# Retention's turned output blocks in two halves, a split third tile, another order in the LRU's last turn, and SiLU as one operation

## The chip, the cores and the metric

The kernel runs on one core of a Trainium2 chip (trn2). The metric is the device time of one execution in microseconds (us). The text speaks of the tensor engine (PE), the vector engine (DVE), the scalar engine (ACT), GpSimd (POOL) and the engine that issues the weight transfers (SP). Each engine takes its instructions in order and waits for the others through semaphores.

## What is computed

Two decoder layers over 1024 tokens of width 1024, all in float32. Layer 0 mixes tokens by retention (4 heads, keys of 256, values of 512), layer 1 by a gated linear recurrence, the LRU (width 1536, 8 gate blocks of 192). Each mixer is followed by a SwiGLU feed-forward part (FFN) of hidden width 2816. Cut to what matters here:

```python
# retention, per head
o = inner + cross                                  # (1024, 512)
o = o * rsqrt(mean(o * o) + eps)
y = (o.reshape(B, S, H * dv) * silu(g)) @ w_out

# recurrence, per channel
gate, u = split(h @ w_in)
u = conv4(u) + conv_b
r = sigmoid(blocks(u) @ w_r + b_r);  i = sigmoid(blocks(u) @ w_i + b_i)
a = exp(-8 * softplus(-lam) * r)
hs = scan(a, sqrt(1 - a * a) * (i * u))            # along the tokens
y = (hs * gelu(gate)) @ w_out

# FFN
y = (silu(h @ w_gate) * (h @ w_up)) @ w_down
```

## The kernel before

**How a product is done.** Float32 accuracy is made of three fast matmuls. Each operand is split into an upper part (`_hi`, a rounded copy) and a lower part (`_lo`, the rest), and `three` (L720 to L728) multiplies hi by hi (L724), lo by hi (L727) and hi by lo (L728) into one PSUM bank. So every operand passes two engines first: for activations ACT copies the upper part and DVE subtracts it from the source, for weights POOL (L531, L533) or ACT and POOL (L1422 or L1433, then L564) do. In the FFN both operands are also combined by sums and differences, so that seven products stand for eight (`H_Q11` to `H_Q21`, `PRODUCTS = 7`).

**Order.** Nothing is scheduled by a planner: the order on each engine is the order in which the code issues the instructions there. Two counting semaphores tie PE to the readers of its eight PSUM banks: `psum_full` counts results that PE has finished, `psum_free` counts results that have been read, and a job numbered e waits until job e - 8 is free (`free`). The reader's count goes up in the order in which DVE works, so PE's numbers must follow DVE's order.

**Retention, per head** (`head`, L886 on PE, L1345 on ACT, L1869 on DVE). PE makes q and k, the gate, the scores, the values, and then eight output blocks o(0) to o(7) of 128 tokens (18 matmuls for the last one). Each block goes to ACT for its sum of squares (L1383) and to DVE for the gate's product (L1943). After four blocks the root is taken (L1391, L1953) and `norm_o` scales the four (L1955). Then PE turns the eight blocks (L964, four 128x128 transposes a block), ACT copies the upper halves (L1395), DVE makes the lower ones (L1969), and the out projection (8 weight units, each 8 blocks of three matmuls) multiplies them. DVE adds its results to the residual (L1867). The last head's out projection is done by halves of the tokens (`out_by_halves`, L762), so that the norm and the transposes of the FFN (L1014, `early_transposes`) can start inside it.

**The recurrence** takes 384 channels a turn, four turns (`GROUPS`). In a turn PE multiplies into u (three tiles of 128 channels by 1024 tokens), into the gate, then the group before's out projection (`lru_outof`), then the gates r and i (`lru_gates`, 84 matmuls). DVE makes the convolution, then the lower half of u (`u_split`, L2272), ACT its upper half (L1648). The gates' results go through `gate_chain` in six items of 512 tokens: sigmoids on ACT (L1658, L1663), `gated` on DVE (L2282), which frees two banks an item, then `scans` (L2290, L2293, the scan itself L2298, the product with the gate branch L2303) in pairs of items, then the split of y (ACT L1690, DVE L2308). In the last turn the out projection of the group before is cut in two: its first column half (8 blocks, 72 matmuls) stands before the gates, its second half behind them; DVE's adds of the second half are placed between the steps of `gate_chain` through `meanwhile`:

```python
scans((2, 3))
meanwhile((0, 1))
y_split((2, 3))
meanwhile((2, 3))
scans((4, 5))
meanwhile((4,))
y_split((4, 5))
meanwhile((5, 6, 7))
```

Then the last group's own out projection follows by halves.

**FFN chunk.** Eleven chunks of 256 hidden columns, two tiles each (`first_tiles_up` for the first chunk of a layer, `tile` for the others). silu(x) is made as sigmoid(x) on ACT (L1445, L1449) and a product x * sigmoid(x) on DVE (L2101 and L2123 in the first chunk, L2165 and L2175 in the others), then a product with the up branch. In the first chunk of a layer ACT also rounds the weights of the down projection, in the same queue as the activations.

## Time and profile before

| what | value |
|---|---|
| median of 3 runs | 2731.73 us (2730.6 to 2732.26) |
| the profiled execution, its own time | 2731.25 us |
| its span in the profile | 2729.4 us |
| PE busy with matmuls | 2677.2 us, 98% of the span |
| DVE, ACT, POOL busy | 1341.4, 824.5, 1251.4 us |
| mean granted PE clock | 0.997 |

The span runs from the first to the last profiled instruction; the 1.85 us between it and the execution's own time lie outside. The profile gives for each engine the time in which it worked and, for each idle stretch, the instruction that ended it. Where PE is busy nearly all the time, the places at which PE waits are the ones to look for; the idle time of the other engines matters only there.

### The profile page before, as it was taken

What the parts mean: (1) busy time and instruction counts of PE and PEld (TensorE: products, weight loads), DVE (VectorE), ACT (ScalarE), POOL (GpSimd) and SP (SyncE); (2) the same over time, 40 slices, a digit from 0 to 9 for tenths busy, and PEclk for the clock granted to TensorE, in tenths of its full rate; (3) what the DMA queues carried; (4) which work ended last, traced back from release to release, by engine and by line L of the source; (5) the groups of instructions that cost most, each with busy time, mean ns of one, the idle gap of its engine ahead of it and who ended that gap; (6) DMA issues with size and microseconds to landing.
All of it is one profiled execution on the core that took longest, in us unless ns stands there. A gap on an engine that the chain in (4) does not pass through costs nothing.

```text
span 2729.4 us, 35372 instructions
## 1 busy us (share of the span) xinstructions
PE 2677.2 (98%) x12017; PEld 2214.7 (81%) x12017; DVE 1341.4 (49%) x1814; ACT 824.5 (30%) x1380; POOL 1251.4 (46%) x1204
## 2 busy tenths in 40 slices
PE   8999999999999999999999999999989999999998
PEld 6888888888888788888888788787877888888886
DVE  8333332323324855555454637356577544545555
ACT  3120120120124433333332524325265222222224
POOL 4323323323323456555555445253454556655554
PEclk9999999999999999999999999999999999999999
DMA  4102102101111111111211111111111111111212
GB/s 141 43 27 65 40 30 64 43 31 60 49 32 43 55 55 46 46 51 55 63 50 56 30 47 49 36 57 36 47 47 47 51 52 52 46 48 54 67 50 81
DMA packets 173624, 139.29 MB, mean 51 GB/s; under 512 B 9184, under 2 KB 143456, under 8 KB 173536
## 3 DMA queue, kind: packets, MB, share of 16 engines
q1 hardware_dynamic: 171440, 133.46, 16.1%
q10 hardware_dynamic: 2096, 4.62, 0.5%
q8 instruction: 59, 0.97, 0.1%
q14 instruction: 29, 0.24, 0.0%
HBM read 132.81 MB, written 5.24 MB: 51 GB/s over the span
## 4 chain that ended last, share of the span: by engine, by line
PE 89%; DVE 6%; ACT 3%; issue 1%; DMA 0%; POOL 0%; POOLq 0%; SPq 0%; DVEq 0%; ACTq 0%
PE ps L724 29%; PE ps L728 29%; PE ps L727 29%; DVE f_h_lo L2016 1%; DVE uc L2298 1%; DVE residual L1867 0%; DVE residual L2211 0%; DVE gate_buf L2303 0%; DVE residual L2369 0%; PE ps L803 0%; DVE h_sum_a L2005 0%; PE ps L865 0%; DVE gate_buf L2090 0%; ACT gate_buf L1237 0%; DVE uc L2293 0%
## 5 line engine op out<-in xcount | busy, mean ns | idle before, releaser
L564 POOL TENSOR_TENSOR f_w_lo<-f_raw,f_w_hi 128x512 fp32r<-128x512 f32 x270 | 354.7, 1318 | 444.5 <-ACT f_w_hi L1422 361.1
L724 PE MATMUL ps<-f_h_hi,f_w_hi 128*128 128x512 f32 x1232 | 481.6, 391 | 3.8 <-DVE f_h_lo L2016 2.1
L728 PE MATMUL ps<-f_h_hi,f_w_lo 128*128 128x512 f32 x1232 | 480.0, 390 | 0.0
L727 PE MATMUL ps<-f_h_lo,f_w_hi 128*128 128x512 f32 x1232 | 480.0, 390 | 0.0
L522 POOL TENSOR_TENSOR small<-w_raw 128x1 f32<-128x1 f32 x200 | 55.4, 277 | 822.7 <-PE ps L724 813.2
L2211 DVE TENSOR_TENSOR residual<-ps,residual 128x512 f32<-128x512 f32 x352 | 239.3, 691 | 157.2 <-PE ps L728 157.2
L724 PEld LDWEIGHTS ps<-f_h_hi,f_w_hi 128*128 128x128 f32 x1232 | 231.3, 188 | 57.8 <-issue 5.1
L724 PE MATMUL ps<-f_w_hi,f_act_hi 128*128 128x512 f32 x688 | 268.4, 390 | 3.0 <-POOL f_w_lo L564 2.8
L728 PEld LDWEIGHTS ps<-f_h_hi,f_w_lo 128*128 128x128 f32 x1232 | 231.3, 188 | 48.1
L727 PEld LDWEIGHTS ps<-f_h_lo,f_w_hi 128*128 128x128 f32 x1232 | 231.4, 188 | 47.0
L727 PE MATMUL ps<-f_w_lo,f_act_hi 128*128 128x512 f32 x688 | 268.0, 390 | 0.0
L728 PE MATMUL ps<-f_w_hi,f_act_lo 128*128 128x512 f32 x688 | 267.9, 389 | 0.0
L533 POOL TENSOR_TENSOR w_lo<-w_raw,w_hi 128x512 fp32r<-128x512 f32 x190 | 257.1, 1353 | 15.2
L1422 ACT ACTIVATE f_w_hi<-f_raw 128x512 fp32r<-128x512 f32 x246 | 154.4, 628 | 338.5 <-PE ps L728 338.4
L724 PE MATMUL ps<-h_hi,w_hi 128*128 128x512 f32 x632 | 248.3, 393 | 3.2 <-DVE uc L2282 3.2
L728 PE MATMUL ps<-h_hi,w_lo 128*128 128x512 f32 x632 | 246.4, 390 | 0.0
L727 PE MATMUL ps<-h_lo,w_hi 128*128 128x512 f32 x632 | 246.4, 390 | 0.0
L564 POOL TENSOR_TENSOR f_w_lo<-f_sum,f_w_hi 128x512 fp32r<-128x512 f32 x124 | 177.8, 1434 | 130.2 <-ACT f_w_hi L1422 122.8
L724 PE MATMUL ps<-w_hi,h_hi 128*128 128x512 f32 x528 | 206.1, 390 | 1.8 <-DVE residual L1867 1.4
L728 PE MATMUL ps<-w_hi,h_lo 128*128 128x512 f32 x528 | 205.7, 390 | 0.0
L727 PE MATMUL ps<-w_lo,h_hi 128*128 128x512 f32 x528 | 205.7, 390 | 0.0
L2163 DVE TENSOR_TENSOR gate_buf<-ps,gate_buf 128x512 f32<-128x512 f32 x120 | 82.8, 690 | 207.8 <-PE ps L728 207.1
(306 smaller groups left out, 4705.4 us busy)
## 6 DMA issues: line engine op xcount, KB each, us to landing
f_raw<-in_ffn_w_gu SPq DMA_DIRECT2D x176, 256.0 KB, 3.4
w_raw<-in_ret_w_in SPq DMA_DIRECT2D x96, 256.0 KB, 2.8
f_raw<-in_ffn_w_down SPq DMA_DIRECT2D x88, 256.0 KB, 2.8
w_raw<-in_lru_w_in SPq DMA_DIRECT2D x48, 256.0 KB, 2.9
w_raw<-in_ret_w_out SPq DMA_DIRECT2D x32, 256.0 KB, 2.6
w_raw<-in_lru_w_out SPq DMA_DIRECT2D x24, 256.0 KB, 2.6
residual<-in_x SPq DMA_DIRECT2D x8, 512.0 KB, 7.2
out_y<-residual SPq DMA_DIRECT2D x8, 512.0 KB, 2.6
```

The costliest lines, as they stand in the source:

```text
L522: nc.gpsimd.tensor_tensor(small[:, 62:63], col, col, ALU.subtract)
L533: nc.gpsimd.tensor_tensor(lo, raw[:, cut], hi.bitcast(F32), ALU.subtract).then_inc(w_ready, 1)
L564: nc.gpsimd.tensor_tensor(lo, src, hi.bitcast(F32), ALU.subtract).then_inc(f_wready, 1)
L724: m = nc.tensor.matmul(o, l_hi, r_hi, start=start, stop=False, skip_group_check=onto)
L727: nc.tensor.matmul(o, l_hi, r_lo, start=False, stop=False, skip_group_check=onto)
L728: return nc.tensor.matmul(o, l_lo, r_hi, start=False, stop=stop, skip_group_check=onto)
L1422: nc.scalar.activation(f_unit(j, last)[0], src, ACT.Copy).then_inc(f_whi, 1)
L2016: TT(H_lo[:, h_cut(form, k)], src[:, t_cut(k)], H_hi[:, h_cut(form, k)].bitcast(F32), ALU.subtract).then_inc(hn_dve, 1)
L2163: TT(t, f_bank(u, p), t, ALU.add).then_inc(f_ev, 1)
L2211: TT(X[:, c], ps[:, b * BANK:(b + 1) * BANK], X[:, c], ALU.add).then_inc(f_ev, 1)
L2298: k = nc.vector.tensor_tensor_scan(uc[:, cut(i)], r_buf[i % 4], uc[:, cut(i)], start, ALU.mult, ALU.add)
```

## The change

There are four parts.

1. **Retention.** PE turns blocks 0 to 3 before the last output block o(7) is summed, and blocks 4 to 7 after the first weight unit has been multiplied with blocks 0 to 3. ACT's and DVE's copies of the turned blocks move with them (`o_turned_upper`, `o_turned_lower`), and the turned blocks lie in `b_hi`/`b_lo` in two pieces (`OT_AT`), so that the first four can be written while scores of the late keys are still read.
2. **u's third tile** is rounded and split in two halves of 512 tokens (`U_PIECES`); the gates wait for the half that they read.
3. **The LRU.** In every turn `gated` of item 2 is issued between the two scans of the first pair. In the last turn only blocks 0 to 3 of the first column half stand before the gates, blocks 4 to 7 and the second half behind them; DVE's adds are placed in two lumps, four before the second pair of scans and eight inside the third pair. The FFN's first four transposes are placed after the third weight unit in both layers; in the LRU's layer, which has three units a half, they stood after the second.
4. **SiLU** is one ACT operation in the FFN; DVE's product with the sigmoid is gone (four instructions a chunk), and so are its semaphore counts. Retention's gate keeps its sigmoid.

```diff
+OT_AT = (0, SCORE_AT[3])
...
+U_PIECES = [(0, 0, S), (1, 0, S), (2, 0, BANK), (2, BANK, S)]
...
+def o_job(s):
+    return J_O + s + (4 if s == SB - 1 else 0)
+def t_job(s):
+    return J_O + s + (SB - 1 if s < 4 else SB)
...
                 pe.wait_ge(s_ready, h * len(SCORES) + len(SCORES))
-                for s in range(SB):
+                def values(s):
                     late = s >= CHUNK
...
-                    if s == 2:
-                        state_sum()
-                for s in range(SB):
-                    free(base + J_T + s)
-                    pe.wait_ge(o_ready, h * 8 + s + 1)
-                    for d in range(4):
-                        m = nc.tensor.transpose(bank(J_T + s, d * P, P),
-                                                R3[:, s * 512 + d * P:s * 512 + (d + 1) * P], ident[:])
-                    m.then_inc(psum_full, 1)
+                def o_turns(blocks):
+                    for s in blocks:
+                        pe.wait_ge(psum_free, base + o_job(s) + 1)
+                        pe.wait_ge(o_ready, h * 8 + s + 1)
+                        for d in range(4):
+                            m = nc.tensor.transpose(bank(J_T + s, d * P, P),
+                                                    R3[:, s * 512 + d * P:s * 512 + (d + 1) * P], ident[:])
+                        m.then_inc(psum_full, 1)
+                for s in range(3):
+                    values(s)
+                state_sum()
+                for s in range(3, SB - 1):
+                    values(s)
+                o_turns(range(4))
+                values(SB - 1)
...
+                        elif (nh, k) == (0, 0):
+                            o_turns(range(4, SB))
...
+                            if j == 0 and s == 4:
+                                o_turns(range(4, SB))
+                            if j == 0:
+                                pe.wait_ge(psum_free, base + t_job(s) + 1)
...
-            def early_transposes(layer, nh, k, nk):
-                if (nh, k) == (0, nk - 2):
+            def early_transposes(layer, nh, k):
+                if (nh, k) == (0, 2):
...
-                            if hf == 0 and m_i == 0 and tile < 2:
-                                pe.wait_ge(u_ready, 3 * g + 2 + tile)
+                            if m_i == 0 and (hf, tile) in ((0, 0), (0, 1), (1, 1)):
+                                pe.wait_ge(u_ready, len(U_PIECES) * g + 2 + tile + hf)
...
-            lru_outof(GROUPS - 2, u0 + 12, base, L_OUT, 0, a_hi, a_lo)
-            lru_gates(GROUPS - 1, base, L_RI_LAST, h_hi, h_lo)
-            lru_outof(GROUPS - 2, u0 + 12, base, L_RI_LAST + 12, 1, a_hi, a_lo)
-            def y_there(half, k):
-                pe.wait_ge(y_ready, (GROUPS - 1) * 6 + half * GT + k + 1)
-            out_by_halves(3, lo, GT, u0 + 18, h_hi, h_lo, y_there, lambda nh, k: early_transposes(1, nh, k, GT))
+            for first in (0, 4):
+                for k in range(GT):
+                    if first == 0:
+                        pe.wait_ge(y_ready, (GROUPS - 2) * 6 + k + 4)
+                        pe.wait_ge(w_ready, u0 + 12 + k + 1)
+                    w = slice(k * 512, (k + 1) * 512)
+                    for s in range(first, first + 4):
+                        e = (L_OUT if first == 0 else L_OUT_LAST - 4) + s
+                        if k == 0:
+                            free(base + e)
+                        c = k * S + s * P
+                        m = three(bank(e), a_hi[:, c:c + P], a_lo[:, c:c + P], w_hi[:, w], w_lo[:, w],
+                                  k == 0, k == GT - 1, s == (4 if k else 0))
+                        if k == GT - 1:
+                            m.then_inc(psum_full, 1)
+                if first == 0:
+                    lru_gates(GROUPS - 1, base, L_RI_LAST, h_hi, h_lo)
+            lru_outof(GROUPS - 2, u0 + 12, base, L_OUT_LAST + 4, 1, a_hi, a_lo)
...
+                    if s == 6:
+                        o_turned_upper(range(4))
...
-                nc.scalar.activation(r3(2 + u), f_bank(u, 0), ACT.Sigmoid).then_inc(f_sig, 1)
-            def sigmoid_2(n, u, first=False):
+                nc.scalar.activation(r3(2 + u), f_bank(u, 0), ACT.Silu).then_inc(f_sig, 1)
+            def silu_2(n, u, first=False):
                 act.wait_ge(f_ev, ev_at(n, u, E_C12, first))
-                nc.scalar.activation(r3(4 + u), r3(7), ACT.Sigmoid).then_inc(f_sig, 1)
+                nc.scalar.activation(r3(4 + u), r3(7), ACT.Silu).then_inc(f_sig, 1)
...
-                gate_o((5, 6, 7))
+                gate_o((5, 6))
+                o_turned_lower(range(4))
+                gate_o((7,))
...
                 def act_2(u):
                     dve.wait_ge(f_sig, 4 * n + 2 + u + 1)
-                    TT(r3(4 + u), r3(7), r3(4 + u), ALU.mult).then_inc(f_ev, 1)
-                    dve.wait_ge(f_ev, ev_at(n, u, E_G2, True))
                     TT(r3(4 + u), r3(4 + u), r3(u), ALU.mult).then_inc(f_act, 1)
...
+            def u_split(g, u_hi, u_lo, pieces=range(len(U_PIECES))):
+                for i in pieces:
+                    tile, a, b = U_PIECES[i]
+                    c = slice(tile * S + a, tile * S + b)
+                    dve.wait_ge(u_rounded, len(U_PIECES) * g + i + 1)
                     TT(u_lo[:, c], uc[:, c], u_hi[:, c].bitcast(F32), ALU.subtract).then_inc(u_ready, 1)
...
+                def scans(items, between=lambda: None, amid=lambda: None):
                     first = step.now()
...
+                    between()
...
+                        if j == 0:
+                            amid()
...
                 gated((0, 1))
-                scans((0, 1))
-                gated((2, 3))
+                scans((0, 1), amid=lambda: gated((2,)))
+                gated((3,))
                 y_split((0, 1))
                 gated((4, 5))
+                meanwhile(0, range(4, SB))
                 scans((2, 3))
-                meanwhile((0, 1))
                 y_split((2, 3))
-                meanwhile((2, 3))
-                scans((4, 5))
-                meanwhile((4,))
+                scans((4, 5), lambda: meanwhile(1, range(SB)))
...
+            def group_before_out(nh, blocks):
                 for s in blocks:
-                    add(base + L_RI_LAST + 12 + s, L_RI_LAST + 12 + s, s, 1)
-            gate_chain(GROUPS - 1, h_hi, h_lo, second_half_out)
+                    e = L_OUT_LAST - 4 + 8 * nh + s
+                    add(base + e, e, s, nh)
```

**The order on PE at the end of a head** (head 0). `b_hi,q_late_lo` is the last matmul of an output block, `ident,gate_buf` are the transposes of the normed blocks, `w_hi,b_hi` is the out projection. Before:

```order
L727 MATMUL ps<-b_lo,q_late_hi 128x512
L728 MATMUL ps<-b_hi,q_late_lo 128x512
L964 MATMUL ps<-ident,gate_buf 128x128 x32
L724 MATMUL ps<-w_hi,b_hi 128x512
L727 MATMUL ps<-w_lo,b_hi 128x512
```

and now (the 18 matmuls of o(7) stand at the first line of dots, three of the four blocks of the unit at the second):

```order
L751 MATMUL ps<-b_hi,q_late_lo 128x512
L983 MATMUL ps<-ident,gate_buf 128x128 x16
L747 MATMUL ps<-a_hi,b_hi 128x512
...
L751 MATMUL ps<-b_hi,q_late_lo 128x512
L747 MATMUL ps<-w_hi,b_hi 128x512
L750 MATMUL ps<-w_lo,b_hi 128x512
...
L983 MATMUL ps<-ident,gate_buf 128x128 x16
L747 MATMUL ps<-w_hi,b_hi 128x512
```

The first 16 transposes have moved ahead of o(7), and 12 matmuls of the first weight unit stand between o(7) and the other 16.

**The order on DVE in the last LRU turn**, from the second pair of scans on (`residual` is an add of the group before, `h_lo` a split of y). Before:

```order
L2290 SCALAR_TENSOR_TENSOR gate_buf<-mask,gate_buf 128x512
L2303 TENSOR_TENSOR gate_buf<-uc,gate_buf 128x512 x2
L1867 TENSOR_TENSOR residual<-ps,residual 128x512 x2
L2308 TENSOR_TENSOR h_lo<-gate_buf,h_hi 128x512 x2
L1867 TENSOR_TENSOR residual<-ps,residual 128x512 x2
L2290 SCALAR_TENSOR_TENSOR gate_buf<-tmp,gate_buf 128x512
...
L2303 TENSOR_TENSOR gate_buf<-uc,gate_buf 128x512 x2
L1867 TENSOR_TENSOR residual<-ps,residual 128x512
L2308 TENSOR_TENSOR h_lo<-gate_buf,h_hi 128x512 x2
L1867 TENSOR_TENSOR residual<-ps,residual 128x512 x11
```

and now:

```order
L1952 TENSOR_TENSOR residual<-ps,residual 128x512 x4
L2369 SCALAR_TENSOR_TENSOR gate_buf<-mask,gate_buf 128x512
...
L2385 TENSOR_TENSOR gate_buf<-uc,gate_buf 128x512 x2
L2390 TENSOR_TENSOR h_lo<-gate_buf,h_hi 128x512 x2
L2369 SCALAR_TENSOR_TENSOR gate_buf<-tmp,gate_buf 128x512
L2369 SCALAR_TENSOR_TENSOR tmp<-gate_buf,tmp 128x512
L1952 TENSOR_TENSOR residual<-ps,residual 128x512 x8
L2373 TENSOR_TENSOR uc<-uc,gate_buf 128x512
```

All eight adds of the second column half now stand ahead of the third pair's products and scans; before, four stood behind them.

**The order on PE inside the last group's out projection** (second half of the tokens; `w_hi` and `lru_out_hi` are weight units, the last `w_hi` row belongs to the second unit, the first `lru_out_hi` row to the third). Before:

```order
L724 MATMUL ps<-w_hi,h_hi 128x512
L727 MATMUL ps<-w_lo,h_hi 128x512
L728 MATMUL ps<-w_hi,h_lo 128x512
L1014 MATMUL ps<-ident,gate_buf 128x128 x16
L724 MATMUL ps<-lru_out_hi,h_hi 128x512
```

and now (the dots stand for the rest of the third unit):

```order
L751 MATMUL ps<-w_hi,h_lo 128x512
L747 MATMUL ps<-lru_out_hi,h_hi 128x512
L750 MATMUL ps<-lru_out_lo,h_hi 128x512
L751 MATMUL ps<-lru_out_hi,h_lo 128x512
...
L1059 MATMUL ps<-ident,gate_buf 128x128 x16
L747 MATMUL ps<-lru_out_hi,h_hi 128x512
```

The 16 transposes have moved back by one unit of 12 matmuls.

## Rows read from the trace of the kernel before

**Rows 1.** The profile's page, part 1: busy us, share of the span, instructions.

```profile
PE 2677.2 (98%) x12017; PEld 2214.7 (81%) x12017; DVE 1341.4 (49%) x1814; ACT 824.5 (30%) x1380; POOL 1251.4 (46%) x1204
```

**Rows 2.** PE's waits in the whole span: us in total, times, longest.

```profile
PE ps L724 <- DVE residual L1867: 6.0, 2, 4.6
PE ps L724 <- POOL f_w_lo L564: 4.8, 5, 1.6
PE ps L964 <- DVE gate_buf L1955: 4.3, 4, 1.1
PE ps L724 <- DVE uc L2282: 4.3, 4, 1.1
...
PE ps L724 <- DVE a_lo L2272: 2.6, 2, 1.3
```

**Rows 3.** Windows: busy us (instructions) in an undisturbed stretch; then the clock, DMA share.

```profile
1100.00:1200.00 100.00, 100.00 (x443) 82.86 (x442) 48.91 (x66) 29.67 (x47) 53.62 (x41) 1.00 0.19 58
```

**Rows 4.** Timeline of PE at head 0's end: start, us, instruction [idle before].

```profile
187.03 1.91 PE L964 MATMUL ps<-ident,gate_buf 128*128 128x128 f32 x16
190.06 1.94 PE L964 MATMUL ps<-ident,gate_buf 128*128 128x128 f32 x16 [1.12 <-DVE gate_buf L1955]
```

**Rows 5.** Timeline of PE at the last head's end.

```profile
832.72 0.47 PE L724 MATMUL ps<-w_hi,b_hi 128*128 128x512 f32 x1 [1.60 <-DVE b_lo L1969]
```

**Rows 6.** Timeline of ACT at head 0's end.

```profile
189.01 4.00 ACT L1395 ACTIVATE b_hi<-ps 128x512 fp32r<-128x512 f32 x8
```

**Rows 7.** Timeline of DVE at head 0's end.

```profile
189.42 1.68 DVE L1955 TENSOR_SCALAR gate_buf<-gate_buf,rstd 128x512 f32<-128x512 f32 x4
191.01 2.48 DVE L1969 TENSOR_TENSOR b_lo<-ps,b_hi 128x512 fp32r<-128x512 f32 x4
```

**Rows 8.** Timeline of DVE, second LRU turn, u's third tile.

```profile
1747.44 1.21 DVE L2272 TENSOR_TENSOR a_lo<-uc,a_hi 128x1024 fp32r<-128x1024 f32 x1
```

**Rows 9.** Timeline of DVE, same turn, items 0 to 2 of the gates.

```profile
1763.29 1.20 DVE L2298 TENSOR_TENSOR_SCAN uc<-gate_buf,uc 128x512 f32<-128x512 f32 x1
...
1765.59 0.69 DVE L2282 TENSOR_TENSOR uc<-uc,xn 128x512 f32<-128x512 f32 x1
```

**Rows 10.** Timeline of ACT, same turn: the second gate of item 2.

```profile
1762.06 0.68 ACT L1663 ACTIVATE xn<-ps,gc_gate 128x512 f32<-128x512 f32 x1
```

**Rows 11.** Timeline of PE in the last group's out projection.

```profile
2019.46 0.76 PE L724 MATMUL ps<-lru_out_hi,h_hi 128*128 128x512 f32 x1 [4.63 <-DVE residual L1867]
```

**Rows 12.** Windows behind that stall.

```profile
2019.40:2024.00 4.60, 4.45 (x10) 3.08 (x11) 4.60 (x8) 2.69 (x7) 4.03 (x3) 0.51 0.00 2
```

**Rows 13.** Timeline of DVE there: the add for which PE waits.

```profile
2018.63 0.68 DVE L1867 TENSOR_TENSOR residual<-ps,residual 128x512 f32<-128x512 f32 x1
```

**Rows 14.** Timeline of ACT ahead of layer 1's FFN: first copy from the fifth transposed tile.

```profile
2043.35 0.69 ACT L1466 ACTIVATE f_h_hi<-ps,cols 128x512 fp32r<-128x512 f32 x1
```

**Rows 15.** Timeline of DVE there: last split, then adds.

```profile
2048.13 0.75 DVE L2005 SCALAR_TENSOR_TENSOR f_h_lo<-ps,cols,f_h_hi 128x512 fp32r<-128x512 f32 x1 [0.41 <-ACT gate_buf L1466]
2048.80 2.47 DVE L1867 TENSOR_TENSOR residual<-ps,residual 128x512 f32<-128x512 f32 x4
```

**Rows 16.** Timeline of DVE, first FFN chunk of layer 0: product with the sigmoid.

```profile
923.51 0.69 DVE L2123 TENSOR_TENSOR gate_buf<-gate_buf 128x512 f32<-128x512 f32 x1
```

**Rows 17.** Timeline of PE there: start of the down projection.

```profile
927.17 0.50 PE L724 MATMUL ps<-f_w_hi,f_act_hi 128*128 128x512 f32 x1 [1.39 <-POOL f_w_lo L564]
```

**Rows 18.** Groups of instructions on ACT: sigmoid and GELU, busy, mean ns.

```profile
L1445 ACT ACTIVATE gate_buf<-ps 128x512 f32<-128x512 f32 x44 | 26.1, 599 | 69.0 <-PE ps L728 68.9
...
L1637 ACT ACTIVATE gate_buf<-ps 128x1024 f32<-128x1024 f32 x12 | 12.3, 1028 | 88.7 <-PE ps L728 88.7
```

**Rows 19.** Timeline of DVE, a later chunk: from the last product to its last split.

```profile
2677.75 0.69 DVE L2172 TENSOR_TENSOR gate_buf<-gate_buf,ps 128x512 f32<-128x512 f32 x1 [1.16 <-PE ps L728]
...
2679.55 1.78 DVE L2175 TENSOR_TENSOR gate_buf<-gate_buf 128x512 f32<-128x512 f32 x1
...
2683.73 1.00 DVE L2183 TENSOR_TENSOR f_act_lo<-gate_buf,f_act_hi 128x512 fp32r<-128x512 f32 x1 [0.70 <-ACT f_act_hi L1454]
```

More of the change, by code:

```diff
@@ L760, in tile_rows, with out_by_halves @@
                 rows_unit(j + 1, u + 1, 1, banks)
-            def out_by_halves(n, extra, nk, u0, l_hi, l_lo, ready, meanwhile):
+            def out_by_halves(n, extra, nk, u0, at, ready, between):
                 for half in range(2):
@@ L770, in out_by_halves @@
                                 pe.wait_ge(w_ready, u0 + j + 1)
-                            if nh == 0:
-                                ready(half, k)
                             w_h, w_l = out_unit(j, extra)
@@ L776, in out_by_halves @@
                                 b = i + (4 * nh if half == 0 else 0)
[L777 to L782 removed]
+                                if nh == 0:
+                                    ready(half, k, i)
+                                if k == 0 and (half or nh):
+                                    pe.wait_ge(psum_free, (e - 4 if half and nh else e - 8) + 1)
+                                m = three(bank(b), *at(half * 4 + i, k), w_h, w_l,
                                           k == 0, k == nk - 1, half == 0 and i == 0)
@@ L785, in out_by_halves @@
                                     m.then_inc(psum_full, 1)
-                            if half:
-                                meanwhile(nh, k)
+                            between(half, nh, k)
             def first_tiles(u0):
@@ L1108, in tile, with down @@
                         product(n, u, p)
-                def down(n, nh, k, s, w, fresh):
-                    if k == 0:
-                        pe.wait_ge(f_ev, fresh)
+                def down(n, nh, k, s, w, added=None, first=False):
+                    if k == 0 and added is not None:
+                        pe.wait_ge(f_ev, added)
+                    elif k == 0:
+                        tile_read(n, s if w is None else 2 * s + nh, first)
                     at = k * S + s * P
@@ L1137, in chunk @@
                         tile(n, 1)
-                    adds = n * F_EV + 2 * PRODUCTS
+                    adds = n * F_EV + 10
                     if last:
@@ L1161, in chunk @@
                                     acted(n, k, s)
-                                m = down(n, nh, k, s, None, adds + s + 1 if nh else tile_read(n, s, first))
+                                m = down(n, nh, k, s, None, adds + s + 1 if nh else None, first)
                                 if k or s == SB - 1:
@@ L1378, in head, with o_turned_upper @@
                 load_sqrt()
+                def o_turned_upper(blocks):
+                    for s in blocks:
+                        full(base + t_job(s))
+                        nc.scalar.activation(o_turned_all(s)[0], bank(J_T + s).rearrange("p (d n) -> p d n", d=4),
+                                             ACT.Copy).then_inc(ot_rounded, 1)
                 for s in range(SB):
-                    full(base + J_O + s)
+                    full(base + o_job(s))
                     if s >= 3:
@@ L1392, in head @@
                             .then_inc(o_root, 1)
-                for s in range(SB):
-                    full(base + J_T + s)
-                    nc.scalar.activation(b_hi[:, 0:4096].rearrange("p (d n) -> p d n", d=4)[:, :, s * P:(s + 1) * P],
-                                         bank(J_T + s).rearrange("p (d n) -> p d n", d=4), ACT.Copy)\
-                        .then_inc(ot_rounded, 1)
+                o_turned_upper(range(4, SB))
             head(0, True)
@@ L1640, in u_round @@
             def u_round(g, base, u_hi, begun=None, full_to=None):
-                for tile in range(GT):
+                for tile, a, b in U_PIECES:
                     if begun is not None and tile < 2:
@@ L1955, in norm_o, with o_turned_lower @@
                         TS(r3(s), r3(s), rstd[:, s:s + 1], None, ALU.mult).then_inc(o_ready, 1)
+                def o_turned_lower(blocks):
+                    for s in blocks:
+                        hi, lo_ = o_turned_all(s)
+                        dve.wait_ge(ot_rounded, h * 8 + s + 1)
+                        TT(lo_, bank(J_T + s).rearrange("p (d n) -> p d n", d=4), hi.bitcast(F32), ALU.subtract)\
+                            .then_inc(psum_free, 1)
                 gate_o(range(3))
```

137 lines of the change are left out of this document (72 added, 65 removed).

## The prediction

> **What bounds the kernel now.** I read the page first: PE works 98% of the span, DVE 49%, ACT 30%, POOL 46% [rows 1]. So PE is the bound, and nothing that shortens another engine's work is worth anything unless PE waits for it. In an undisturbed stretch a matmul starts every 0.227 us (443 records touch 100 us, two of them only in part) [rows 3]. The number of 512-column matmuls does not change, so the change can only win or lose PE's idle time, 52 us in all (2729.4 - 2677.2). Next I read the list of PE's waits [rows 2]: it names five that the change touches. They are 6.0 us for adds to the residual, 4.3 us for the normed output blocks, 4.3 us for `gated` (L2282), 2.6 us for the lower part of u's third tile, and part of the 4.8 us for a weight's lower part from POOL. Last came the timelines around each. An idle figure counts from the modelled end of the matmul before; seen from start to start each stop costs some 0.1 us more, because the first matmul behind it is slower (0.50 instead of 0.39 us for one, as in [rows 17]).
>
> **Retention's turns.** At the end of a head PE turns 16 tiles and can turn the next 16 only 3.03 us after the first (187.03 to 190.06) [rows 4]; 16 transposes need 1.78 us by their pitch of 0.11, so 1.25 us are lost. The chain in that time is o(7)'s square, mean, root and `norm_o` (DVE, 189.42) [rows 7], and it starts when o(7) is complete. Now 12 matmuls, 12 x 0.227 = 2.72 us, stand between o(7) and the second turn, so 3.03 - 2.72 = 0.3 us remain. Then block 4 must be copied: PE needs 0.5 us for it, ACT copies at 0.50 us a block (8 in 4.00) [rows 6], DVE splits at 0.62 (4 in 2.48) but only behind its four `norm_o` [rows 7], which end 1.04 us after the second turn begins. That gives about 2.05 us against the 1.78 of the turn: 0.3 us of a new wait, and 0.1 for the extra stop. The next blocks come at 0.62 us on DVE and are used at 0.68 (three matmuls). The first turn, ahead of o(7), needs `norm_o` of blocks 0 to 3, which ended while o(5) was summed; its copies (4 x 0.5 on ACT, 4 x 0.62 on DVE) lie beside the 18 matmuls of o(7), 4.1 us, and ahead of o(7)'s square on ACT. So three heads win 1.25 - 0.7 = 0.55 us each, 1.6 in all. In the last head PE also waits 1.60 us for the lower parts of four blocks, 1.75 by starts [rows 5]; that goes wholly, since blocks 4 to 7 are used only in the other half: 1.25 + 1.75 - 0.4 = 2.6. Together **4.2 us**; bounds are 2 (every head finds a wait of 0.6 more) and 5.5 (no new wait).
>
> **u's third tile.** In turns 2 and 3 PE waits 1.3 us for one split of 1024 columns, 1.21 us long, behind DVE's adds [rows 2, 8]. A half takes 0.62 to 0.69 [rows 7, 9], so PE goes on 0.5 us earlier: **1.0 us** in the two turns, bounds 0 and 1.2. The second half is read 42 matmuls later and costs nothing. ACT's extra instruction hides behind the adds.
>
> **`gated` inside the scans.** After the gates PE waits four times 1.1 us, once in each turn, for item 2's product [rows 2]: it ran at 1765.59, behind the second scan (1763.29) and two products [rows 9]. Its input was there at 1762.06 + 0.68 = 1762.74 [rows 10]. Now it starts when the first scan ends, at 1763.29, which is 2.3 us earlier; the wait of 1.2 us is gone in the three inner turns, 3.7 us. In the last turn the two blocks that follow take only 1.36 us, then PE needs item 3's product, which runs when it did: some 0.3 us come back, 0.9 are won. **4.6 us**, bounds 3 and 4.9. y of items 0 and 1 comes 0.6 us later and nobody waits for it.
>
> **The last turn.** PE stood 4.63 us (and 1.4 us before that, together 6.0) for adds of the second column half [rows 2, 11]: the add stood behind the third pair's scans and products and ran at 2018.63 [rows 13]. After that the granted clock was 0.51, the lower level (1.2 GHz), and 10 matmuls took 4.6 us instead of 2.3 [rows 12]. Now blocks 4 to 7 of the first half (4 blocks x 3 units x 3 = 36 matmuls, 8.2 us) have gone from ahead of the gates to behind them, and all eight adds stand ahead of the third pair's products. The results of the second half are complete 3 to 0.1 us before PE wants their banks; DVE is done with the second pair by then, and adds one in 0.62 us (4 in 2.47) [rows 15] against PE's 0.68 a block. I take all of it as won: 6.0 + 2.3 + 0.3 for two restarts = **8.6 us**; bounds 4 (half of the wait and the clock's part stay) and 9.
> What bears on the clock's 2.3 us: the Trainium skill's page "TensorE: Matmul & The Clock Gate", section "What's actually happening", says that the throttled state is the default and activity releases it, so without the stop the slow matmuls go too. By it the sum is the same only while no stop of that length remains here; if one did, its slow stretch would stay, which is what the bound of 4 says.
> Ahead of the gates the out projection now covers only 8.2 instead of 16.3 us of u's rounding and splitting. They need some 6 us (one GELU, 1.03 [rows 18], and u's first two tiles at 1.0 to 1.2 on each engine), so nothing is added.
>
> **The FFN's first transposes, layer 1.** They move back by one unit, 2.72 us, while the products behind them stay. ACT copies, squares and copies again without a gap, so its first copy of the fifth tile (2043.35) [rows 14] moves by 2.72; so does DVE's last split (2048.13) and the first add behind it (2048.80, ready at 2049.42) [rows 15]. PE wants that bank for the FFN's first product 0.5 us after that. So PE waits 2.2 us there, and since ACT's chain behind it (squares, root, scaling, first terms) sets the next turns too, the full shift comes out: **-2.7 us**. Bounds: 0 (if the chain has slack that I missed) and -3.5.
>
> **SiLU.** No such operation is in the trace. Its nearest rows are the sigmoid (599 ns for 512 columns) and GELU (1028 ns for 1024) [rows 18]; I take 0.6 us and bound it by 0.5 and 1.3. The Trainium skill's "ScalarE: Activation LUTs", section "What ACT_TABLE_LOAD costs", says one element a cycle for every function; by that it costs what the sigmoid costs, and the sum stands as it is. In the chunks of the loop PE does not wait, so 0.69 to 1.78 us less on DVE [rows 16, 19] buy nothing. In the first chunk of each layer they do: PE's 1.39 us [rows 17] were for a weight whose rounding stands on ACT behind the activation that needs the product of [rows 16]. One product less on that chain (0.7 with its wait) and another ahead of it on DVE (0.2, since then the matmul's result binds) give 0.95, and a wait of 0.2 to 0.3 behind it goes: 1.15 a layer, **2.3 us**; bounds 0.8 and 3.2. The last 20 us of the kernel are DVE's adds and the final norm, and are not touched.
>
> **Sum.** 4.2 + 1.0 + 4.6 + 8.6 - 2.7 + 2.3 = 18.0 us. The profiled execution took 2731.25, the median is 0.5 more. 2731.25 - 18.0 = 2713.25; for the median **2713.5 us**.
>
> **Rivals.**
> - *The later transposes cost nothing.* For it: DVE idles 0.41 us ahead of each split there [rows 15]. Against: it idles for ACT, which has no gap in that stretch. Then 2713.5 - 2.7 = 2710.8. Chance 0.12.
> - *The last turn keeps a stall.* DVE is the only engine for 12 adds, 3 splits and the third pair; if POOL's weight splits stretch its products (0.69 against 1.78 [rows 16, 19]), y or a bank is late again, say by 3 us, and the clock falls too (2.3): 2713.5 + 5 = 2718.5. For it: this stretch had such products before. Against: the adds, which PE needs, read PSUM and took 0.62. The Trainium skill's "SBUF — State Buffer", section "SBUF: two separate sides", calls the port of DVE and GpSimd an exclusive lock; a loser waits for a whole operation of the other. Chance 0.14.
> - *The early turns give their gain back* on the copies of blocks 4 to 7, or o(7) starts late: the first term falls from 4.2 to 1: 2716.7. Chance 0.08.
> - *Slower: SiLU is long.* In a later chunk DVE's last split ends at 2684.73, 6.98 us after the product's result [rows 19]; PE wants it 36 matmuls, 8.16 us, after the product, so about 1.0 us is free, and 1.6 to 2.7 with one product less. A SiLU beyond 2.3 to 3.4 us stops PE at the end of every chunk. To undo 18 us and 5.5 more in some 20 chunks it needs 1.2 us beyond that, 3.5 us or more: six times the sigmoid. At 4.6 us with the larger slack: 2713.5 + 20 x 1.2 = 2737.5. Chance 0.02.
> - *The change does not do what it says*: the order of the built programs shows the moved transposes, adds and `gated`, and the same number of table loads on ACT. Under 0.01.
>
> **The numbers.** The forecast has 0.64. About 0.2% (5.5 us) is what a measurement of this kernel can tell from no change. All cases but the slow SiLU lie over 10 us below 2731.73: faster 0.97, same 0.01, slower 0.02. The low end takes in the first rival and 1.5 us of the other bounds, the high end the second: 2709 to 2719.
>
> **What would show it.** PE's list of waits without `gated`, and with at most 0.4 us a head for L1955's successor; no window with a clock near 0.5 behind the last group's out projection; a new wait of about 2.2 us of the FFN's first product for an add to the residual in layer 1, and none in layer 0; 0.5 us or so left at the start of the first down projection; SiLU at 0.6 us. I am wrong if PE still waits over 3 us for one add in the last turn, if the first product of layer 1 does not wait, or if SiLU's mean is over 1.3 us.

## The result and the profile after

| | before | changed |
|---|---|---|
| median of 4 runs | 2731.84 us (2730.6 to 2732.26) | 2715.01 us (2714.54 to 2716.61) |
| profiled execution | 2731.25 us | 2714.54 us |
| its span | 2729.4 us | 2712.7 us |

The ratio is 0.994 with a 95% interval of 0.9923 to 0.9957: the change makes the kernel 16.8 us faster. The forecast was 2713.5 us with a range of 2709 to 2719. The total lies in the range, but it was not reached by the terms as they were given: one of them, the third largest, was nearly lost, and others came out larger.

The page's busy row of the changed kernel, for [rows 1]:

```profile
PE 2673.3 (99%) x12017; PEld 2212.2 (82%) x12017; DVE 1274.1 (47%) x1730; ACT 826.6 (30%) x1384; POOL 1259.5 (46%) x1204
```

PE's matmuls are the same in number and take 3.9 us less, mostly since ten of them no longer run at the slow clock [rows 12]. DVE lost 67 us of work that nobody waited for, apart from the first chunks.

PE's waits in the changed kernel, for [rows 2] (engine, what waits, line; what ended the wait; us in total, times, the longest):

```profile
PE ps L983 <- DVE gate_buf L2040: 4.5, 5, 1.0
...
PE ps L747 <- DVE a_lo L2351: 1.6, 2, 0.8
PE ps L747 <- DVE residual L1952: 1.5, 1, 1.5
...
PE ps L747 <- POOL f_w_lo L587: 0.6, 2, 0.3
PE ps L1059 <- DVE h_sum_a L2093: 0.6, 1, 0.6
...
PE ps L747 <- DVE uc L2361: 0.2, 1, 0.2
PE ps L1059 <- DVE f_h_lo L2093: 0.2, 1, 0.2
```

Of the five waits of [rows 2] four have shrunk, about as forecast: `gated` (now L2361) from 4.3 to 0.2, adds to the residual from 6.0 to a single new one of 1.5 us, u's lower part from 2.6 to 1.6, POOL's lower parts from 4.8 to 0.6 (of these, one stop of 1.80 us in the last chunk only changed its name: it is 1.89 now and put down to ACT's SiLU). The fifth has not: the wait for the normed output blocks (L2040, the successor of L1955) is 4.5 us in total, where it was 4.3.

The table splits the 16.7 us of span. A stop is counted from start to start ("by starts"): it is what two neighbouring matmuls take beyond 0.227 us, or two transposes beyond 0.13. "By the shift" means how much earlier the same instruction starts in the one trace than in the other; it also holds what lies between the stops.

| part | forecast | stops before | stops after | won |
|---|---|---|---|---|
| retention's turns | 4.2 | 1.26 + 1.17 + 1.17 + 1.26, and 1.74 in the last head | 1.15 + 1.05 + 1.06 + 1.15, three times 0.24 behind the turn, 0.92 + 0.22 in the last head | 0.3 (0.7 by the shift) |
| u's third tile | 1.0 | 2 x 1.47 | 2 x 0.94 | 1.1 |
| `gated` | 4.6 | 1.25 + 1.24 + 1.17 + 1.26 | 0.41 | 4.5 |
| the last turn | 8.6 | 1.57 + 4.79, and 2.7 by the slow clock | none | 9.1 |
| FFN's first transposes, layer 1 | -2.7 | 0.49 | 0.37 + 1.64 + 0.77 | -2.3 |
| SiLU | 2.3 | 2 x (0.34 + 1.55 + 0.24) | 2 x 0.48 | 3.3 to 3.5 |

The sum is 16.0 to 16.6. The head ends are where the forecast and the trace part. Here is the first head's end on DVE and POOL, where [rows 7] shows the end of the same chain before the change:

```profile
189.82 0.75 DVE L2028 SCALAR_TENSOR_TENSOR gate_buf<-ps,gam,gate_buf 128x512 f32<-128x512 f32 x1 [2.70 <-ACT tmp L1470]
190.49 1.00 DVE L2032 TENSOR_SCALAR ssq<-ssq 128x4 f32<-128x4 f32 x1
191.83 0.18 DVE L2038 RECIPROCAL rstd<-rstd 128x4 f32<-128x4 f32 x1 [0.34 <-ACT rstd L1480]
192.05 1.68 DVE L2040 TENSOR_SCALAR gate_buf<-gate_buf,rstd 128x512 f32<-128x512 f32 x4
```
```profile
189.48 0.61 POOL L554 CAST w_hi<-w_raw 128x512 fp32r<-128x512 f32 x1
190.18 1.29 POOL L556 TENSOR_TENSOR w_lo<-w_raw,w_hi 128x512 fp32r<-128x512 f32 x1
```

DVE's mean over four columns (L2032) took 1.00 us and ended at 191.49, just behind POOL's subtraction (190.18 + 1.29 = 191.47); it is 1.00 us in each of the four heads. Before the change it took 0.16:

```profile
188.71 0.16 DVE L1947 TENSOR_SCALAR ssq<-ssq 128x4 f32<-128x4 f32 x1
```
```profile
192.59 0.61 POOL L531 CAST w_hi<-w_raw 128x512 fp32r<-128x512 f32 x1
```

There POOL's split of that weight unit began at 192.59, behind the chain, because PE began the out projection only then; a unit's split starts when PE begins the unit two before it. The change lets PE begin the out projection right behind o(7), and with it POOL's split moved into DVE's chain. In the last head POOL goes on to further units, and `norm_o` is held up too:

```profile
831.26 3.04 DVE L2040 TENSOR_SCALAR gate_buf<-gate_buf,rstd 128x512 f32<-128x512 f32 x4
```

against 1.68 us for the same four in the first head. That gives the stop of 0.92 us between two turned blocks: the second of the four scalings alone took 1.49 us beside POOL's next subtraction, where one takes 0.48 by itself.

The last turn of the LRU is as forecast: behind the 0.41 us for `gated` there is no stop up to the FFN's transposes, and the granted clock stays at 1.00. Three windows of PE (stretch, length, busy us and instructions, granted clock, DMA share, GB/s), for [rows 12]:

```profile
2009.00:2014.00 5.00, 5.00 (x24) 1.00 0.00 0
2014.00:2019.00 5.00, 5.00 (x24) 1.00 0.00 0
2019.00:2024.00 5.00, 5.00 (x32) 1.00 0.01 3
```

### The profile page after: what moved, and what is told of

It reads as the page before. It is cut to its first block, busy times and chain, and to the rows that moved or that the text cites. A ratio compares the mean times of both kernels' runs of the same rounds, so it can differ in the third digit from the quotient of the medians.

```text
span 2712.7 us, 35233 instructions
## 1 busy us (share of the span) xinstructions
PE 2673.3 (99%) x12017; PEld 2212.2 (82%) x12017; DVE 1274.1 (47%) x1730; ACT 826.6 (30%) x1384; POOL 1259.5 (46%) x1204
## 4 chain that ended last, share of the span: by engine, by line
PE 92%; DVE 4%; ACT 2%; issue 1%; DMA 0%; POOL 0%; SPq 0%; DVEq 0%; ACTq 0%
PE ps L747 30%; PE ps L750 30%; PE ps L751 30%; DVE f_h_lo L2104 1%; PE ps L983 0%; ACT gate_buf L1318 0%; DVE residual L2289 0%; DVE residual L2451 0%; PE ps L823 0%; DVE h_sum_a L2093 0%; DVE gate_buf L2178 0%; DVE residual L1952 0%; DMA residual<-in_x 0%; ACT f_h_hi L1556 0%; DVE f_h_lo L2093 0%
```

## The experiments

Each starts from the changed kernel. Stops are by starts.

### 1. POOL held back in the heads

```diff
+                    if j == HEAD_UNITS - 6:
+                        pool.wait_ge(o_ready, h * 8 + 8)
                     split(slot, ...)
```

> The changed kernel, with one wait more: POOL starts the split of the out projection's third unit in each head only when the last of the eight normed blocks is there. In the changed kernel PE still loses 1.15, 1.05, 1.06 and 1.15 us ahead of the second turn, and the last head 0.92 and 0.22 us more inside it. Theory (the mean of the squares on DVE, 1.00 us instead of 0.16, and in the last head norm_o, 3.04 instead of 1.68, are held up by POOL's cast and subtraction that now lie beside them): the mean falls back to 0.16 us, norm_o to 1.68, PE loses 0.3 us ahead of each second turn and nothing inside the last head's; 4 x 0.85 + 1.1 = 4.5 us less, 2710.5 us. Rival (it is the later start of the chain, or PE's own restart, and POOL only happens to run there): the mean stays at 1.0 us or PE's stop stays at 1.05 to 1.15 us, time 2715 +- 1. Third way: POOL's later splits come too late for PE, new waits for w_lo behind the turn, slower than 2715.

Measured: 2710.82 us (2710.02 to 2711.83), 4.2 less than the changed kernel; ratio to before 0.9922 (0.9905 to 0.9939). The same chain in the last head, and POOL's first cast there:

```profile
828.03 0.16 DVE L2034 TENSOR_SCALAR ssq<-ssq 128x4 f32<-128x4 f32 x1
828.53 0.18 DVE L2040 RECIPROCAL rstd<-rstd 128x4 f32<-128x4 f32 x1 [0.34 <-ACT rstd L1482]
828.74 1.68 DVE L2042 TENSOR_SCALAR gate_buf<-gate_buf,rstd 128x512 f32<-128x512 f32 x4
```
```profile
830.63 0.61 POOL L554 CAST w_hi<-w_raw 128x512 fp32r<-128x512 f32 x1
```

The mean is back at 0.16 and `norm_o` at 1.68 us. PE's stops ahead of the second turn are 0.31, 0.22, 0.21 and 0.31 us, and no stop is left inside the last head's turn. The forecast's "0.3 us remain" was right for a chain without POOL. No wait for a weight appeared. By the shift the heads are 4.6 us shorter; the profiled span fell by 3.0 only, because 0.9 us were lost at the kernel's start and 0.8 from there to the LRU's entry, where the clock was low for longer (0.50 in both windows of 3 us from 1545 us on; 0.66 and 0.77 in the two from 1548 us on in the changed kernel, which gets there 3.7 us later). Nothing was edited at either place. One wait on POOL, which changes nothing else, brings back what this part lacked, so POOL's work beside DVE's chain had taken it. The Trainium skill's page "SBUF — State Buffer", section "SBUF: two separate sides", says that DVE and GpSimd share one pair of ports as an exclusive lock, taken by DVE operations in a two-port mode or with two inputs from SBUF. The traces agree for DVE's operations from SBUF to SBUF: 1.00 against 0.16 us, ending with POOL's operation; in which mode DVE ran them no run here shows. DVE's adds, which read PSUM, keep 0.69 us beside POOL (L1952, 673 to 693 ns in all its 128).

### 2. More cover in the last head instead

```diff
-                        elif (nh, k) == (0, 0):
+                        elif (nh, k) == (0, 1):
                             o_turns(range(4, SB))
```

> The changed kernel, with the last head's second turn behind two units of the out projection instead of one (12 matmuls, 2.72 us, more cover); the three first heads as they were. Theory (the second turn lacks cover for a chain that is 1.0 us longer than thought): the last head's 1.15 + 0.92 + 0.22 us go, those of the first three heads stay at 1.05 to 1.15; 2.2 us less, 2712.8 us. Rival (the copies of the blocks or the banks of the turned blocks then hold up the third unit or the fifth): part of it comes back as a wait for a bank or for b_lo, 2713.5 to 2715.

Measured: 2712.77 us (2712.29 to 2713.11), 2.2 less. All three stops of the last head are gone, while DVE is as slow as in the changed kernel:

```profile
829.86 0.99 DVE L2032 TENSOR_SCALAR ssq<-ssq 128x4 f32<-128x4 f32 x1
831.19 0.18 DVE L2038 RECIPROCAL rstd<-rstd 128x4 f32<-128x4 f32 x1 [0.34 <-ACT rstd L1480]
831.41 3.06 DVE L2040 TENSOR_SCALAR gate_buf<-gate_buf,rstd 128x512 f32<-128x512 f32 x4
```

The other heads kept 1.14, 1.06 and 1.04. So the collision can also be covered instead of removed; where the copies of the later blocks are needed late, 12 more matmuls cost nothing.

### 3. The FFN's first transposes of layer 1 back in their old place

```diff
-                if (nh, k) == (0, 2):
+                if (nh, k) == (0, 2 - layer):
```

> The changed kernel, with the FFN's first transposes of layer 1 one unit (2.72 us) earlier again, where the kernel before had them; layer 0 untouched. Theory (their later place costs what PE loses at 2026.5, 2032.7 and in part at 2045.8: 0.37 + 1.64 + 0.28 = 2.3 us): these three go and nothing takes their place, 2712.7 us. Rival (DVE's scaling of the eight half rows runs only from 2015.9 to 2021.6 us, 0.72 us each beside POOL's products, and PE would ask for the first four at 2018.0): PE waits 0.8 us or more for gate_buf at the first of these transposes, and one to two of the 2.3 us come back: 2714 to 2715.

Measured: 2714.54 us (2714.29 to 2716.54), no difference; the span is the same to the last digit, 2712.7. PE's waits show the exchange:

```profile
PE ps L1059 <- DVE gate_buf L2080: 2.0, 1, 2.0
...
PE ps L1059 <- DVE h_sum_a L2093: 0.3, 1, 0.3
```

The 1.5 us for the add are gone, and 2.0 us (2.21 by starts) stand ahead of the first transpose, for the rows that DVE scales. The rival holds: the late place alone does not explain the loss of 2.3 us.

### 4. SiLU undone

```diff
-                nc.scalar.activation(r3(2 + u), f_bank(u, 0), ACT.Silu)
+                nc.scalar.activation(r3(2 + u), f_bank(u, 0), ACT.Sigmoid)
...
+                TT(r3(2 + u), f_bank(u, 0), r3(2 + u), ALU.mult)
```

> The changed kernel, with SiLU undone (sigmoid on ACT, product on DVE, as before); the rest as changed. Theory (SiLU is worth only what PE loses in the first chunk of each layer): PE's stops of 0.34, 1.55 and 0.24 us come back there in place of one of 0.48, in both layers, 1.65 a layer, 3.3 us in all, 2718.3 us; the chunks of the loop show no new wait. Rival as predicted before the result: 1.15 a layer, 2717.3 us. Second rival (the loop's chunks had hidden waits that the product of 0.69 to 1.78 us made longer): more than 5 us, 2720 or above.

Measured: 2719.92 us (2718.57 to 2720.22), 4.9 more, where 3.3 were expected. The stops came back as 0.36, 1.58 and 0.25 us in place of 0.48 and 0.47, in both layers: 3.4 us, or 3.8 by the shift of the instructions behind them. In the profiled execution, 5.7 us longer in span, another 1.4 lie where SiLU has no part, behind the last head's turn, because the clock fell there (PE windows):

```profile
832.00:834.00 2.00, 0.90 (x6) 0.95 0.36 131
834.00:836.00 2.00, 2.00 (x11) 0.50 0.52 131
836.00:838.00 2.00, 2.00 (x9) 0.70 0.37 116
```

In the changed kernel the same windows have 1.00 throughout. The remaining 0.5 us lie at the kernel's start. Whether the clock fell in the three other executions too is not on record, so the median's 4.9 us cannot be split as surely. By the profiled pair SiLU is worth 3.3 to 3.8 us, all of it in the first chunks; the loop's chunks show no new stop, so the second rival falls although the median comes near its 5 us. How long the operation is could be read in the changed kernel's groups (busy us, mean ns), for [rows 18]:

```profile
L1534 ACT ACTIVATE gate_buf<-gate_buf 128x512 f32<-128x512 f32 x44 | 27.5, 625 | 8.4 <-DVE gate_buf L2252 5.5 <-DVE gate_buf L2202 2.9
L1530 ACT ACTIVATE gate_buf<-ps 128x512 f32<-128x512 f32 x44 | 26.1, 598 | 69.0 <-PE ps L751 68.9
```

598 ns from PSUM, where the sigmoid had 599 [rows 18]: the slow rival is out. The Trainium skill's "ScalarE: Activation LUTs", section "What ACT_TABLE_LOAD costs", says that every function takes one element a cycle; the two equal times agree with it.

### 5. The last turn's order undone

```diff
-            for first in (0, 4):
...
+            lru_outof(GROUPS - 2, u0 + 12, base, L_OUT, 0, a_hi, a_lo)
+            lru_gates(GROUPS - 1, base, L_RI_LAST, h_hi, h_lo)
...
-                meanwhile(0, range(4, SB))
                 scans((2, 3))
+                meanwhile((0, 1))
                 y_split((2, 3))
-                scans((4, 5), lambda: meanwhile(1, range(SB)))
+                meanwhile((2, 3))
+                scans((4, 5))
+                meanwhile((4,))
                 y_split((4, 5))
+                meanwhile((5, 6, 7))
```

> The changed kernel, with the last turn's order as before (all eight blocks of the first half ahead of the gates, the eight adds of the second half in pieces around the third pair); SiLU, the halves of u, gated inside the scans and the transposes' new place stay. Theory (as the prediction had it: 6.0 us of waits for adds and 2.3 of slow clock behind them are what this part won): PE stops again some 1.5 us for a bank behind the second half, then about 4.8 us for one add behind the third pair's products, and the granted clock falls to about 0.5 for some 5 us behind it. Between the gates and the first product of the FFN 8.6 us more; but the 2.3 us that PE now loses at the FFN's first transposes and first product were measured with the stall gone, so up to 2.3 us of them can go: 2721.3 to 2723.6 us. Rival (the granted clock falls by itself, not from the stop): the stop comes back with a clock of 1.0 behind it, 2 us less, 2719 to 2721. Second rival (the transposes one unit later or gated's new place already mend this stop): no stop over 1 us there, 2715 to 2716.

Measured: 2726.13 us (2724.94 to 2726.94, 10 runs), 11.1 more than the changed kernel; the profiled spans differ by 10.4. That is above the expected range. PE's wait for adds and the windows behind the long stop:

```profile
PE ps L747 <- DVE residual L1937: 7.6, 3, 4.7
...
PE ps L747 <- DVE uc L2346: 0.9, 2, 0.7
```
```profile
2005.00:2010.00 5.00, 2.50 (x12) 1.00 0.69 180
2010.00:2015.00 5.00, 2.73 (x6) 0.51 0.01 2
2015.00:2020.00 5.00, 5.00 (x19) 0.80 0.00 0
```

The stops are 1.57 and 4.84 us, and the slow matmuls behind them cost 2.8 by the shift: 9.2, against the forecast's 8.6. The rest is an effect of two parts together. The stops for `gated` in this turn grow from 0.41 to 1.48 us (0.41, 0.86 and 0.21): with eight blocks a unit behind the gates PE asks for the banks of items 3, 4 and 5 one after the other; with four blocks a unit it asks for those of items 4 and 5 two units later. And the stop at the FFN's first product stayed (1.65), so nothing was given back. Both rivals fall: in this run too the clock was low right behind the long stop (0.51), and neither the later transposes nor `gated` mends the stop.

### 6. u's halves and `gated` undone

```diff
-U_PIECES = [(0, 0, S), (1, 0, S), (2, 0, BANK), (2, BANK, S)]
+U_PIECES = [(0, 0, S), (1, 0, S), (2, 0, S)]
...
-                scans((0, 1), amid=lambda: gated((2,)))
-                gated((3,))
+                scans((0, 1))
+                gated((2, 3))
```

> The changed kernel, with two parts undone at places that lie apart: u's third tile whole again, and gated behind both scans and products. Theory: PE's two stops ahead of the gates' third tile go from 0.94 back to 1.47 us (1.06 in all, the half split being 0.6 us shorter), and four stops of 1.2 us for item 2's product come back in place of one of 0.41 (4.5 us): 5.6 us more, 2720.6 us. Rival for the last turn (there the stop of gated had been hidden in the old order's later stall and now it only moves y): 0.4 us more or less than that. Rival for u (the second half, not the first, holds PE up): the stops stay at 0.94 us and the sum is 4.5, 2719.5 us.

Measured: 2721.12 us (2720.78 to 2722.77), 6.1 more.

```profile
PE ps L747 <- DVE uc L2361: 4.2, 4, 1.1
...
PE ps L747 <- DVE a_lo L2351: 2.6, 2, 1.3
```

By starts the third tile's stops are 1.47 twice (0.53 more each), and `gated` stops PE for 1.25, 1.25, 1.17 and 1.17 us instead of 0.41 once: 5.5 us, as expected for both, and 5.8 by the shift. The rest of the profiled difference (0.5 us) lies ahead of the LRU, where nothing was edited.

### 7 and 8. POOL held back in layer 1, without and with the transposes' old place

```diff
                 lower(0, 4, raws[0][3])
+                if layer:
+                    pool.wait_ge(hx_dve, layer * HX_DVE + 8)
                 sum_1(1)
```

The eighth experiment has this and the edit of the third.

> The changed kernel, with one wait more: in layer 1 POOL makes the sums of the second tile's weights only when DVE has scaled the eight half rows of the FFN's norm (in the changed kernel both lie together, and the eight take 5.78 us instead of 3.26). The transposes stay where the change put them. Theory (two bounds stand close together, the late transposes and the slow scaling, and lifting one alone gives nothing): the scaling falls to about 3.3 us, the stops at 2026.5 and 2032.7 stay at 0.37 and 1.64 us, 2715 +- 0.7. Rival (the scaling alone is what makes PE wait there): the stops go, 2712.7 us. Third way (POOL's sums then come too late): new waits for f_w_lo in the first chunk of layer 1, 2716 or more.

> As the kernel before in this list, and the FFN's first transposes of layer 1 one unit (2.72 us) earlier again. Moving them alone gave nothing: PE's 2.0 us for the add were replaced by a stop of 2.21 us for DVE's scaled half rows. Theory (that stop is POOL's doing: its sums lie beside DVE's scaling): the first four rows are there at about 2017.5 us, ahead of PE at 2018.0, no stop over 0.3 us at the transposes and none at the first product: 2.3 us less than the changed kernel, 2712.7 us. Rival (the rows would come too late anyway, since their squares and root end at 2015.9): a stop of 1 to 2 us stays at the transposes, 2714 to 2715.

Measured: 2715.49 us (2714.98 to 2716.28) and 2713.48 us (2712.82 to 2714.49). DVE's scaling of the eight half rows, in the changed kernel, in the seventh and in the eighth experiment:

```profile
2015.86 5.78 DVE L2080 TENSOR_SCALAR gate_buf<-residual,rstd 128x512 f32<-128x512 f32 x8
```
```profile
2016.39 3.26 DVE L2082 TENSOR_SCALAR gate_buf<-residual,rstd 128x512 f32<-128x512 f32 x8
```
```profile
2016.89 3.26 DVE L2082 TENSOR_SCALAR gate_buf<-residual,rstd 128x512 f32<-128x512 f32 x8
...
2020.23 1.29 POOL L590 TENSOR_TENSOR f_sum<-f_raw 128x512 f32<-128x512 f32 x1 [3.94 <-DVE gate_buf L2082]
```

With the late transposes the faster scaling gives nothing: the stops are 0.49 and 1.64 us. With the early ones no loss is left: no stop at the transposes, none at the first product, and the stretch from the last turn's stop for `gated` to the stop at the first half's sums falls from 73.55 us (1972.29 to 2045.84) to 71.25 (1973.32 to 2044.57), 2.3 us. The median fell by 1.5. So two bounds of nearly the same size stood there. Each hid the other: the third and the seventh experiment, which lift one each, show no gain beyond the spread of the runs.

### 9 and 10. Together, and u's half ahead of the last add

The ninth takes the edits 1, 3 and 7 together; the tenth adds, in the inner turns:

```diff
                 for s in range(SB):
+                    if s == SB - 1:
+                        u_split(g, a_hi, a_lo, (2,))
                     add(base + L_OUT + 8 + s, L_OUT + 8 + s, s, 1)
-                u_split(g, a_hi, a_lo, (2, 3))
+                u_split(g, a_hi, a_lo, (3,))
```

> The changed kernel with POOL held back at the two places where it lay beside DVE's work from SBUF to SBUF (behind the normed blocks in each head, behind the scaled half rows in layer 1), and the FFN's first transposes of layer 1 one unit earlier. Theory (the two gains are independent, one being in the heads and one at the FFN of layer 1): 4.2 as measured for the first plus 2.3 by PE's starts for the second (1.5 by the medians): 2708.5 to 2709.5 us, about 2709. Rival (part of the gains was the clock's or a neighbour's luck): 2711 or above.

> As the kernel before in this list, and DVE splits the first half of u's third tile ahead of the last of the eight adds in turns 2 and 3, where PE still loses 0.94 us each. Theory (the half is one add of 0.62 us too late; ACT has rounded it 1.5 us before): both stops go to 0.3 us, 1.2 us less, about 2707.8 us. Rival (the last add, now 0.6 us later, frees the bank that a gate wants, so that the stop moves): the stops stay near 0.9 us in sum, 2709.

Measured: 2708.76 us (2707.77 to 2709.07), ratio 0.9917 (0.9903 to 0.993), and 2707.67 us (2707.03 to 2707.77), ratio 0.9912 (0.9899 to 0.9926). The gains add up. In the tenth the third tile's stops are 0.34 us twice instead of 0.95, and the later add stops nobody:

```profile
1739.15 0.67 DVE L2355 TENSOR_TENSOR a_lo<-uc,a_hi 128x512 fp32r<-128x512 f32 x1
1739.75 0.68 DVE L1956 TENSOR_TENSOR residual<-ps,residual 128x512 f32<-128x512 f32 x1
1740.35 0.67 DVE L2355 TENSOR_TENSOR a_lo<-uc,a_hi 128x512 fp32r<-128x512 f32 x1
```

It is the fastest kernel of this document: 23.7 us under the kernel before (2731.36 measured beside it) and 7.3 under the changed one.

## Why the prediction was right, and where it was not

The total was right within 1.5 us, and in part that is luck. Retention's turns gave 3.5 to 3.9 us less than forecast; SiLU (1.0 to 1.2), the last turn (0.5) and the FFN's first transposes (0.4) gave some 2 more, and that closed half of the gap.

- **Retention's turns** (4.2 forecast, 0.3 to 0.7 measured) was wrong, and the failing step is "so 3.03 - 2.72 = 0.3 us remain". It took the chain's 3.03 us from [rows 4, 7] as fixed and moved only the cover. But PE's earlier start of the out projection releases POOL's next split, and with it the mean of 0.16 us becomes one of 1.00; in the last head `norm_o` grows from 1.68 to 3.04. The prediction's own sign for this term, at most 0.4 us a head for L1955's successor, failed: it was 1.0. The prediction had the third rival, "the early turns give their gain back", at 0.08 and with the copies as the cause; the term did fall to 1 or less, but by POOL. It named the shared port as a danger for the last turn of the LRU only. The copies themselves cost what was said or less: the 0.3 us of a new wait for block 4 did not appear, only 0.24 us for the restart behind the turn. With POOL held back the part is worth 4.2 us more by the medians (4.6 by the shift), so the rest of the reasoning on the cover held.
- **u's third tile** (1.0) and **`gated`** (4.6) were right: 1.1 and 4.5. The 0.3 us that were to come back in the last turn for item 3 are there, 0.41. That they are no more is owed to the new order of the out projection (experiment 5: 1.48 in all with the old one).
- **The last turn** (8.6) was right in its mechanism and measured 9.1: the slow stretch with its restarts cost 2.7 us, where the terms for both were 2.3 and 0.3, and the stops were 6.4 us by starts instead of 6.0. The opening sentence, that the change can only win PE's idle time, left out these slow matmuls, which count as busy; the sum did have them. The rival of a remaining stall fell: the adds read PSUM, and none of them took over 0.69 us, beside POOL or not.
- **The FFN's first transposes** (-2.7) was right in size (-2.3) and incomplete in its cause. The wait of PE's first product for an add came as described, 1.5 us where 2.2 were forecast. But the rival "costs nothing" and the forecast both took DVE's scaling for granted, which lasted 3.26 us before; it had become 5.78 beside POOL's sums, so that the old place would have cost the same. Before the change the scaling began at 2032.48, 1.7 us after POOL's last sum. Without the stall it begins at 2015.86, 16.6 us earlier, while POOL's last sum ends only 11.4 us earlier (2019.37): what was won ahead of it moved one engine's work into another's.
- **SiLU** (2.3) was too small: 3.3 to 3.5. POOL's stop fell by 1.07 us a layer (0.95 forecast), and the two small stops of 0.34 and 0.24 us around it, for which "0.2 to 0.3" stood, went wholly. Of these the prediction had no term for the one ahead. The operation's length was right, 0.60 and 0.63 us against 0.6.

## What to carry to other kernels

When an engine's start is moved earlier, list what it releases, on every queue: here the split of a weight unit that POOL begins when PE begins an earlier unit moved with it, into DVE's chain. When lifting one bound gives nothing, a second bound of equal size may stand behind it, so lift both together before you call a part worthless. A correct total is no proof of the terms; only the stops one by one showed that about a fifth of the expected gain was missing here.

## What the runs showed of the hardware

- POOL's cast and subtraction, both from SBUF to SBUF, stretch DVE's short operations from SBUF: a mean over 128x4 from 0.16 to 1.00 us, four scalings of 128x512 from 1.68 to 3.04, eight from 3.26 to 5.78. The mean of 0.16 us lost 0.84 us, nearly as much as a single scaling of 0.48 us (1.49 in the last head, 1.51 in layer 1), which is what matters in a chain of short steps. DVE's adds from PSUM kept 0.67 to 0.69 us.
- The same two stops in the last head (1.15 and 0.92 us) were followed by a clock of 1.00 in the profiled executions of the changed kernel and of experiments 3, 5, 6, 7 and 8, and by one of 0.50 for over 3 us in experiment 4. The 4.8 us stop was followed by 0.51 in both kernels that have it. Where the clock fell it cost 1.4 us beyond the short stops and 2.7 to 2.8 beyond the long one. Behind the 3.1 us stop at the LRU's entry it fell in all twelve kernels, and longer in experiments 1 and 2 than in the changed kernel. Why it fell behind the same stops in one execution and not in the others stays open.
